# Softmax denominators of the second layer as eight one-column products in a PSUM slot of the ring

## What is computed

```python
def block_attention(q, k, v, scale):
    def one_block(qblk):
        s = jnp.einsum('bqkgd,blkd->bkgql', qblk, k).astype(jnp.float32) * scale
        p = jax.nn.softmax(s, axis=-1).astype(v.dtype)
        return jnp.einsum('bkgql,blkd->bqkgd', p, v)
...
def hybrid_layer(xl, xc, c, c_ctx, p, lam_init, tabs64, tabs32, ctx_out):
    ...
    o_a = block_attention(ql_a, jnp.concatenate([kc_a, kl_a], 1), jnp.concatenate([vc_a, vl_a], 1), GQA_SCALE)
    ...
    y_l = merge_groups(o_a, o_b, o_m, ga_l, gb_l, gc_l, p["w_out"])
    xl_new = layer_norm(DEEPNORM_ALPHA * xl + gt_l[:, None, :] * y_l, p["ln_g"], p["ln_b"])
    if not ctx_out:
        return xl_new, None
    ...
```

## Time and profile before

| | us |
|---|---|
| Median of 3 runs | 947.19 |
| Lowest and highest | 946.35, 947.42 |
| Time of the profiled execution | 949.86 |
| Span of the profiled execution | 948.0 |
| TensorE busy in it | 908.3 |
| DVE, POOL, ScalarE busy in it | 557.3, 511.1, 429.8 |

### The profile page before, as it was taken

How to read it: one execution, slowest core, us unless ns; L and a number is a source line. 1 busy time by engine, 2 the same in 40 slices (tenths; PEclk the granted TensorE clock), 3 DMA queues, 4 the chain that set the end, 5 groups by cost and what they waited for, 6 DMA issues and landing times.

```text
span 948.0 us, 13381 instructions
## 1 busy us (share of the span) xinstructions
PE 908.3 (96%) x4629; PEld 641.7 (68%) x4629; DVE 557.3 (59%) x903; ACT 429.8 (45%) x879; POOL 511.1 (54%) x433
## 2 busy tenths in 40 slices
PE   5999999999999999999999899999999999999996
PEld 3778667889744565665678779888884445555684
DVE  5569033523678679963318838567246758983337
ACT  5332121414556466655334853235335645655432
POOL 3247223324577755565547438455538886566672
PEclk9999999999999999999999999999999999999998
DMA  9957662213623200010353212222343221020242
GB/s 318 291 214 261 211 249 75 73 45 100 142 53 92 60 18 18 18 68 1 129 189 112 98 31 82 86 65 84 79 120 78 69 50 26 18 76 1 104 164 88
DMA packets 51913, 96.13 MB, mean 101 GB/s; under 512 B 9540, under 2 KB 24752, under 8 KB 50824
## 3 DMA queue, kind: packets, MB, share of 16 engines
q1 hardware_dynamic: 51848, 95.29, 32.7%
HBM read 71.61 MB, written 4.21 MB: 80 GB/s over the span
## 4 chain that ended last, share of the span: by engine, by line
PE 79%; DVE 8%; ACT 6%; issue 2%; POOL 2%; DMA 1%; SPq 1%; POOLq 0%; ACTq 0%; DVEq 0%
PE banks L1003 14%; PE banks L1005 13%; PE banks L1004 13%; PE banks L1300 12%; PE banks L1322 11%; PE banks L1245 4%; ACT area_z L1859 2%; PE banks L1014 2%; PE banks L1341 2%; DVE negmax L2254 2%; PE banks L1274 1%; PE banks L1334 1%; DMA w_raw<-in_w_in_dram 1%; ACT late_bias L1836 1%; DVE area_b L2431 1%
## 5 line engine op out<-in xcount | busy, mean ns | idle before, releaser
L1968 POOL TENSOR_TENSOR w_split<-w_raw,w_split 128x512 fp32r<-128x512 f32 (+4 forms) x122 | 148.7, 1226 | 217.1 <-ACT w_split L1577 215.4
L1003 PE MATMUL banks<-w_split,area_a 128*128 128x512 f32 (+3 forms) x612 | 232.1, 379 | 5.7 <-issue 2.7
L1005 PE MATMUL banks<-w_split,area_a 128*128 128x512 f32 (+3 forms) x612 | 224.7, 367 | 0.0
L1004 PE MATMUL banks<-w_split,area_a 128*128 128x512 f32 (+3 forms) x612 | 224.0, 366 | 0.0
L2254 DVE TENSOR_REDUCE negmax<-banks 128x1 f32<-128x768 f32 x160 | 148.2, 951 | 79.1 <-PE banks L1245 55.8
L1577 ACT ACTIVATE w_split<-w_raw 128x512 fp32r<-128x512 f32 (+4 forms) x122 | 69.1, 582 | 195.4 <-PE banks L1005 185.9
L1695 ACT ACTIVATE area_z<-banks 128x512 f32<-128x512 f32 x196 | 108.3, 599 | 75.9 <-PE banks L1300 72.7
L1003 PEld LDWEIGHTS banks<-w_split,area_a 128*128 128x128 f32 x612 | 115.3, 188 | 38.8 <-issue 21.2
L1300 PE MATMUL banks<-area_a 97*128 97x512 f32 (+4 forms) x448 | 128.4, 401 | 4.2 <-ACT area_z L1695 3.1
L1005 PEld LDWEIGHTS banks<-w_split,area_a 128*128 128x128 f32 x612 | 115.2, 188 | 16.5
L1004 PEld LDWEIGHTS banks<-w_split,area_a 128*128 128x128 f32 x612 | 115.6, 189 | 12.8
(11 more groups left out here) (238 smaller groups left out, 1443.2 us busy)
## 6 DMA issues: line engine op xcount, KB each, us to landing
w_raw<-in_w_in_dram SPq DMA_DIRECT2D x32, 512.0 KB, 3.6
area_g<-in_w_ada_dram SPq DMA_DIRECT2D x13, 1024.0 KB, 6.3
area_g<-in_w_ada_dram SPq DMA_DIRECT2D x16, 512.0 KB, 5.9
w_raw<-in_w_out_dram SPq DMA_DIRECT2D x16, 512.0 KB, 4.3
area_a<-parts SPq DMA_DIRECT2D x72, 96.0 KB, 2.2
area_a<-parts SPq DMA_DIRECT2D x30, 192.0 KB, 3.6
area_b<-in_x_dram SPq DMA_DIRECT2D x8, 512.0 KB, 7.6
w_raw<-in_w_in_dram SPq DMA_DIRECT2D x8, 352.0 KB, 5.5
```

What stands on the lines that cost most here:

```text
L1003: nc.tensor.matmul(dst, a[0], b[0], start=first, stop=False)
L1004: nc.tensor.matmul(dst, a[0], b[1], start=False, stop=False)
L1005: return nc.tensor.matmul(dst, a[1], b[0], start=False, stop=last)
L1968: op = nc.gpsimd.tensor_tensor(lo, raw, hi.bitcast(F32), ALU.subtract)
```

## The change

In the second layer only, the three steps of the denominators become one. `column_sums` takes each total as the stationary operand, 128 queries at a time, and streams one column of ones: 4 blocks x 2 units = 8 products, each of which writes one column of 128 partitions, so that the queries stand on the partitions at once. ScalarE's copy and the four transposes go, and the DVE takes the reciprocals from the eight columns. The group stands where the transposes stood, behind score step 3; nothing stands between score steps 2 and 3 any more. The ring has one entry less a pair: "d" takes the place of "dt", and its slot is free again when the reciprocals are taken. The first layer keeps its instructions.

```diff
@@ the ring's order
-        if last:
+        if last and ctx:
             RING += [("d", _L, _p - 1)]
         if now:
             RING += [("s", _L, _p, 3, u) for u in range(2)]
         if last:
-            RING += [("dt", _L, _p - 1)] + [("o", _L, _p - 1, g) for g in ((1, 0) if ctx else (1,))]
+            RING += [("dt" if ctx else "d", _L, _p - 1)] + [("o", _L, _p - 1, g) for g in ((1, 0) if ctx else (1,))]
@@ ring_ready
-                    elif k[0] == "d":
+                    elif k[0] == "d" and k[1] < DEPTH - 1:
                         pe.wait_ge(d_copied, PN[k[1:]] + 1)
-                    elif k[0] == "dt":
+                    elif k[0] in ("d", "dt"):
                         pe.wait_ge(rec_done, PN[k[1:]] + 1)
@@ TensorE
+            def column_sums(L, p):
+
+                pe.wait_ge(dve_summed, N_DVE_SUM[L, p, 1])
+                dst = ring_slot("d", L, p)
+                for i in range(TILES - CT):
+                    for u in range(2):
+                        mm = nc.tensor.matmul(dst[:, 2 * i + u:2 * i + u + 1], total(L, p, u)[:, i * P:(i + 1) * P],
+                                              ones_c[:, 0:1], start=True, stop=True)
+                mm.then_inc(ring_filled, 1)
...
-                    denominators(L, p - 1)
+                    if context:
+                        denominators(L, p - 1)
                     if context:
                         max_rows(L, p + 1, "ctx")
                     scores(L, p, 3)
                     max_tile(L, p + 2, 0)
-                    turn_denominators(L, p - 1)
+                    if context:
+                        turn_denominators(L, p - 1)
+                    else:
+                        column_sums(L, p - 1)
                     turn_output(L, p - 1)
...
                 if context:
                     mix(L, p, "ctx")
-                denominators(L, p)
+                if context:
+                    denominators(L, p)
                 out_step(L, 1, latents)
-                turn_denominators(L, p)
+                if context:
+                    turn_denominators(L, p)
+                else:
+                    column_sums(L, p)
                 turn_output(L, p)
@@ ScalarE (the same in the last pair and behind it)
                     exponent(L, p, 2)
-                    copy_denominators(L, p - 1)
+                    if context:
+                        copy_denominators(L, p - 1)
                     exponent(L, p, 3)
@@ VectorE, output_rows
+                else:
+                    r = N_RINGB["d", L, p] - 1
+                    dve.wait_ge(ring_filled, r + 1)
+                    nc.vector.reciprocal(rec[:, 0:2 * len(ts)], banks[:, r % NRING, 0:2 * len(ts)]).then_inc(rec_done, 1)
```

More of the change, by code:

```diff
@@ L1341, in denominators @@
                     mm = nc.tensor.matmul(dst[32 * u:32 * u + 32, :], ones_c[:], total(L, p, u), start=True, stop=True)
-                if L < DEPTH - 1:
-                    for u in range(2):
-                        mm = nc.tensor.matmul(dst[64 + 32 * u:96 + 32 * u, :], ones_c[:], prob(L, p, "ctx", u), start=True, stop=True)
+                for u in range(2):
+                    mm = nc.tensor.matmul(dst[64 + 32 * u:96 + 32 * u, :], ones_c[:], prob(L, p, "ctx", u), start=True, stop=True)
                 mm.then_inc(ring_filled, 1)
@@ L1348, in turn_denominators @@
                 pe.wait_ge(d_copied, PN[L, p] + 1)
-                rows = P if L < DEPTH - 1 else 64
                 dst = ring_slot("dt", L, p)
                 for i in range(TILES - CT):
-                    mm = nc.tensor.transpose(dst[:, i * P:i * P + rows], d_rows[0:rows, i * P:(i + 1) * P], ident[0:rows, 0:rows])
+                    mm = nc.tensor.transpose(dst[:, i * P:(i + 1) * P], d_rows[:, i * P:(i + 1) * P], ident[:])
+                mm.then_inc(ring_filled, 1)
[3 more added lines that the diff above has]
+                for i in range(TILES - CT):
+                    for u in range(2):
+                        mm = nc.tensor.matmul(dst[:, 2 * i + u:2 * i + u + 1], total(L, p, u)[:, i * P:(i + 1) * P],
+                                              ones_c[:, 0:1], start=True, stop=True)
                 mm.then_inc(ring_filled, 1)
@@ L1719, in copy_denominators @@
                 act.wait_ge(ring_filled, r + 1)
-                copy(d_rows[0:rows, :], banks[0:rows, r % NRING, :]).then_inc(d_copied, 1)
+                copy(d_rows, banks[:, r % NRING, :]).then_inc(d_copied, 1)
             def squares(L, p):
@@ L2302, in output_rows @@
                     nc.vector.reciprocal(rec[:, 0:2 * CT].rearrange("p (t u) -> p t u", u=2), d_s[:])
-                nc.vector.reciprocal(rec[:, k - 2 * (TILES - CT):k].rearrange("p (t u) -> p t u", u=2),
-                                     turned[:, :, 0:2, 0]).then_inc(rec_done, 1)
+                    nc.vector.reciprocal(rec[:, 2 * CT:2 * TILES].rearrange("p (t u) -> p t u", u=2),
+                                         turned[:, :, 0:2, 0]).then_inc(rec_done, 1)
+                else:
+                    r = N_RINGB["d", L, p] - 1
+                    dve.wait_ge(ring_filled, r + 1)
+                    nc.vector.reciprocal(rec[:, 0:2 * len(ts)], banks[:, r % NRING, 0:2 * len(ts)]).then_inc(rec_done, 1)
                 dve.wait_ge(rec_done, n + 1)
```

12 lines of the change are left out of this document (6 added, 6 removed).

## The result

The changed kernel takes 962.69 us (median of 4 runs, 959.68 to 964.11), the kernel before 946.95 us (4 runs, 946.35 to 947.42). The ratio is 1.0151, with a 95% interval of 1.0133 to 1.017: 1.5% slower, 15.7 us. The forecast was 955.0, in a range of 949.5 to 963.5.

The account below looks back on a forecast made before the run. TensorE was taken as the bound, holding 79% of the chain. The median 947.2 us plus 4.1 without the clock and 3.7 for clock falls gave 955.0 us, range 949.5 to 963.5.

Parts of the forecast that it names:

- case A: Second layer's attention: one to four more clock falls, 952.9 to 957.7 us, middle 955.0; chance 0.40.
- case B: The new group drops the clock nearly everywhere: five to nine more falls, 959.3 to 965.7 us; chance 0.23.
- without the clock: Sum of the seven places (+1.7 us) and the three with a wait (+2.4 us): +4.1 us.
- The score steps side by side: Score steps 2 and 3 with nothing between take 2.09 us with two passes, 3.00 with three.
- The loads: Sixteen f32 weight loads of 128 columns a place, 0.11 us each, 1.76 us; bounds 0.06 and 0.19 us each.
- Rival D: Loads don't overlap the products, 0.19 us each: 964.1 us before any fall; chance 0.05.
- rival E: The group is cheaper than what goes, loads at the transposes' 0.06 us: 943.3 us; chance 0.04.
- The seven places: Where the chain is TensorE from end to end: 1.80 us comes, 1.56 goes, +0.24 each, +1.7 us together.
- The three places with a wait: Near 726, 796 and 817 us, where TensorE waits for ScalarE: +0.5, +0.93 and +0.93, together +2.4 us.
- SP's later release: SP's wait for the last denominators ends some 3.5 us later; covered by some 10 us, so nothing.
- The clock: Two or three more falls of TensorE's clock, first behind the waits: 2.3 x 1.6 = +3.7 us.
- case C: No more clock falls than before, as weight loads may count as work: 950.2 to 952.4 us; chance 0.22.

Follow-up runs that it names:

- the doubled group: The changed kernel with 64 streamed columns instead of one and its group of products run twice, thirty-two loads: 977.09 us, ratio 1.0309.
- that with 64 columns: The changed kernel with each of the eight products streaming 64 columns of ones instead of one, same place behind score step 3: 956.34 us, ratio 1.0091.
- the table's three late profiles: Pair lengths with the group behind score step 3: changed kernel (962.69 us), its unedited rerun (963.13 us), and 64 streamed columns instead of one (956.34 us).
- the second profile: Profile of the changed kernel run once more with no edit: 963.13 us, ratio 1.0162.
- the early place: The changed kernel with its eight products moved back between score steps 2 and 3, where L1341 stood: 957.45 us with one column, 947.51 us with 64.
- The wait with one product behind it: The changed kernel with one product of eight columns in place of the eight products, the others left out of the denominators: 940.36 us, ratio 0.9922.
- fill the rest first: The kernel before, its second layer's products with ones using all four column groups of the array and two full transposes replacing four: 943.63 us, ratio 0.9954.

## Why the forecast was right in its direction and short in its size

**The number and its parts.** 962.69 us lies in the range, but not in the forecast's own case A, which ended at 957.7; the range reached it because it held most of case B. The two halves of the forecast missed in opposite directions: without the clock I had +4.1 us, where the parts below give some +2, and for the clock +3.7, where 13 to 14 of the 15.7 us remain. So the distance of 7.7 us hides how short the clock term was.

**The score steps side by side: right.** 2.10 us measured, 2.09 forecast, and the 3.00 with three passes was right too (L1300 x12 takes 3.00 us on the changed kernel's chain at 867.94).

**The loads: right.** 0.112 us each. Rival D (0.19) and rival E (0.06) fall. The Trainium skill's 81 ns for a load and its matmul ("TensorE: Matmul & The Clock Gate", "Back-to-back issue gap") is stated for 128 streamed columns and names no data type. It does not carry over to these f32 loads: the doubled group says 112 ns, with 64 columns.

**The seven places: mis-sized, +1.7 us forecast.** Six of them have a pair without low clock, in the changed kernel's two profiles or, for one of them, in that with 64 columns, and these are between 0.05 us longer and 0.19 us shorter than before, about -0.2 us in sum. What I had wrong is the edge of the group. The loads of this place in the timeline of the changed kernel:

```profile
757.12 1.24 PEld L1300 LDWEIGHTS banks<-area_a 128*128 128x128 f32 x6 [0.25 <-issue]
...
759.10 1.86 PEld L1361 LDWEIGHTS banks<-ones_c,w_raw 128*128 128x128 f32 x16 [0.25 <-issue]
```

and of the kernel before:

```profile
757.61 0.77 PEld L1300 LDWEIGHTS banks<-area_a 128*128 128x128 f32 x4 [0.26 <-issue]
...
761.25 0.42 PEld L1334 LDWEIGHTS banks<-ident,o_t 128*128 128x128 f32 x4
```

From the first load of step 2 to that of the output's transposes it is 3.64 us before (757.61 to 761.25) and 3.68 after (757.12 to 760.80). The score steps now hold 1.98 of it and the group 1.70. So 3.64 - 1.98 = 1.66 us goes, where I had 1.56, and 1.70 comes, where I had 1.80: the loads begin behind the matmuls ahead of them, and the transposes' loads begin behind the last of the group. +0.04 a place, not +0.24.

**The three places with a wait: right as far as they could be measured.** At 796 the first score products of step 3 run early and the other waits 1.58 us, as forecast. At 726 the wait for the copy is gone. From the first load of step 2 to that of the transposes it was 3.01 us (725.87 to 728.88) and is 3.57 (723.55 to 727.12): +0.56, forecast +0.5. No profile of the changed kernel kept the clock in the pairs of 796 and 817, so the +0.93 can only be bounded. When half of the low clock is taken off each pair's growth, at least 1.1, 0.9 and 1.1 us are left at 796 in the table's three late profiles, and 0.75, 1.1 and 1.0 at 817. That agrees with +0.93.

**SP's later release: right, nothing.** The tail is as long as before (50.5 us in both), although x is loaded 3.5 us later with respect to the transposes.

**The clock: the step that failed.** I forecast 2.3 more falls at a fixed 1.6 us, +3.7. The profiled run had 23.8 instead of 6.6 us at the low clock. Over the whole span (1 - mean clock) x span is 15 us in it and 18 to 22 us in the other three runs, against 8 us in the profiled run of before and 4 to 9 in its later ones.

The number of falls was nearly right: four instead of two, in both profiles, at four of the ten places, and the two with a wait are among them, as I had said. What I had wrong is their length, and so their price. Both falls of before last 3.4 us, and I took 1.6 us for one. In the changed kernel the fall at 798 lasts 6.8 us (10.2 in the second profile) and the one at 822 lasts 10.2 (6.8). By the time and by the us at the low clock this is case B (959.3 to 965.7), which had 0.23; but B's condition, a fall nearly everywhere, did not come. The stretches of the changed kernel's first profile, cut at the two long falls:

```profile
790.00:797.80 7.80, 5.14 (x20) 2.19 (x19) 7.66 (x10) 6.53 (x13) 3.94 (x3) 1.00 0.00 0
797.90:804.70 6.80, 6.80 (x29) 5.62 (x30) 2.48 (x5) 0.66 (x2) 2.99 (x3) 0.50 0.00 0
804.80:821.70 16.90, 14.58 (x62) 7.92 (x58) 16.16 (x18) 10.84 (x21) 9.41 (x7) 1.00 0.11 25
821.80:832.00 10.20, 10.02 (x34) 6.19 (x34) 5.74 (x9) 1.47 (x4) 5.21 (x4) 0.50 0.00 0
```

They show the order too. The clock is low from 797.9 on and the first load of the group starts at 798.05; it is low from 821.8 on and the group starts at 822.92. So here the clock fell ahead of the group, behind 1.58 us in which TensorE waited for ScalarE, and while the group ran it stayed down. In the second profile the first of the two falls comes ahead of the group too (low from 797.2, group from 798.07), the second 0.45 us into it. At the two-pass and three-pass places it is the other way round: the falls near 743 and 853 follow a group (741.10 to 742.8, 849.54 to 851.3).

The price of the group also depends on the clock, which the forecast did not carry. The two loads of the earlier trace rows, from which I took 0.11 us, stand where the clock was full again. At the low clock the sixteen loads take 3.64 us in place of 1.86. That this longer group is what keeps the clock down is my reading and not shown by itself.

One row was misread as well. For case C I said that the clock returns between 797.5 and 800.8. The mean of 0.80 in that row is a fall that begins in it, and the stretch right behind it in the kernel before is wholly at the low clock:

```profile
799.50:802.90 3.40, 3.40 (x13) 1.59 (x13) 2.71 (x5) 0.27 (x1) 2.83 (x3) 0.50 0.00 1
```

So what I gave as the reason for C is not in the record.

That the number of streamed columns makes the difference, with the same loads, is shown by two pairs of kernels that on TensorE differ in nothing else: 1 and 64 columns at the late place, 962.69 and 956.34 (ratios to before 1.0151 and 1.0091), and at the early place 957.45 and 947.51 (1.0097 and 1.0005; mean clocks 0.980 to 0.983 and 0.992 to 0.996). The place matters beside it: 64 columns late still cost 8.8 us more than 64 columns early. What sets off the falls at 796 and 817 stays open. The wait with one product behind it kept the clock in its profile, and so did the group of 64 columns inside the wait; the wait with the whole group behind it lost it in all four profiles of that order (the changed kernel's two, 64 columns, and the doubled group). That fits a joint cause, but the kernel before also lost the clock behind the wait at 796 (for 3.4 us, from 799.5), without the group.

## What to carry to other kernels

Before a step is turned into many stationary loads with few streamed columns, count what TensorE streams in that stretch: here a group about as long as what it replaced made the kernel 1.5% slower, most of it by the clock. Where the output has room, try letting each load stream more columns than are needed: 64 hid behind the next load here. Put such a group into a wait that is there anyway. The two together brought this kernel back to the time of before, not below it. Where products use a part of the array's columns, fill the rest first: that gave 4 us here.

## What the runs showed of the hardware that I had not expected

- TensorE can be busy in the records without a gap for 40 us and still have its clock fall (0.87 over 740 to 780 us in the kernel with the early group), where the records hold groups of many loads and one streamed column.
- Weight loads of 128 columns of f32 follow each other every 0.112 us at the full clock. At the low clock, with one or with 64 columns streamed behind each, sixteen take 3.64 us, 0.22 us each.
- 64 streamed columns of f32 cost nothing behind such a load: pairs of 15.67, 16.92 and 17.76 us with 1 and with 64 columns alike.
- The same program's runs spread by 4.4 us (959.68 to 964.11) when its clock falls often, and by 1.1 us (946.35 to 947.42, 4 runs) or 2.8 us (946.39 to 949.17, 13 runs) in the kernel before, so runs of such a kernel are compared through the clock in each.
- The low clock can cost less where TensorE waits anyway. Of the kernel with the early group and one column, the pair with the wait near 800 is 1.6 us longer than with 64 columns, for 5.1 us at the low clock (22.48 and 20.88). A pair that TensorE bounds is 2.6 us longer for 6.4 us (19.76 and 17.13).
